# C scores over full rows with the low keys in both row halves, and the first pass's bias rows read three weight loads later

## What is computed

```python
h = jnp.einsum('bsd,de->bse', x, w_in)
a_out = pool_mixer(a_v, a_group_w, a_scale) * jax.nn.silu(a_gate)
b_out = swa_sink_attention(b_q, b_k, b_v, b_sinks) * jax.nn.silu(b_gate)
c_out = chunk_relbias_attention(c_q, c_k, c_v, c_rel_bias) * jax.nn.silu(c_gate)
y = jnp.einsum('bse,ed->bsd', jnp.concatenate([a_out, b_out, c_out], -1), w_out)
x = layer_norm(alpha * x + y)
```

```python
s = jnp.einsum('bnqhd,bnkhd->bnhqk', qc, kb) * (C_HEAD_DIM ** -0.5)
s = jnp.where(valid, s + bias, NEG_INF)
o = jnp.einsum('bnhqk,bnkhd->bnqhd', softmax(s), vb)
```

## Time and profile before

| | us |
|---|---|
| median of 3 runs | 3065.4 |
| profiled execution, its own time | 3064.84 |
| its span, first to last instruction | 3063.1 |
| TensorE busy | 2966.9 (97%) |
| VectorE busy | 1396.8 (46%) |
| ScalarE busy | 1202.5 (39%) |
| GpSimd busy | 1285.9 (42%) |
| mean granted clock of TensorE | 0.986 |

### The profile page before, as it was taken

The page is one execution under the profiler, slowest core; times in us unless marked ns, Lnnn a source line. Parts: engine busy times, 40 slices in busy tenths (PEclk is TensorE's granted clock), DMA queues, the critical chain, the costliest instruction groups (busy, mean ns, idle before and its releaser), DMA issues.

```text
span 3063.1 us, 46760 instructions
## 1 busy us (share of the span) xinstructions
PE 2966.9 (97%) x14272; PEld 2459.6 (80%) x14272; DVE 1396.8 (46%) x2483; ACT 1202.5 (39%) x2543; POOL 1285.9 (42%) x942
## 2 busy tenths in 40 slices
PE   7999999999999999999999999999999999999995
PEld 6777888888777878888878788888887777888884
DVE  4343455422556555541155555552126556555204
ACT  4333445422433444542234344553224444444321
POOL 4333444444434334444444444444443343444445
PEclk9999999999999999999999999999999999999998
DMA  5323322354433322235444442224553343222343
GB/s 174 99 91 107 103 83 81 98 170 157 146 130 124 117 89 80 82 95 163 158 153 138 136 136 86 79 80 140 162 179 104 97 134 130 83 79 79 101 125 142
DMA packets 187768, 360.68 MB, mean 118 GB/s; under 512 B 19072, under 2 KB 27296, under 8 KB 184352
## 3 DMA queue, kind: packets, MB, share of 16 engines
q1 hardware_dynamic: 185952, 346.99, 36.3%
q10 hardware_dynamic: 1728, 12.58, 1.0%
HBM read 319.63 MB, written 43.02 MB: 118 GB/s over the span
## 4 chain that ended last, share of the span: by engine, by line
PE 89%; issue 5%; DVE 4%; ACT 1%; POOL 1%; DMA 0%; SPq 0%; POOLq 0%; ACTq 0%; DVEq 0%
PE acc L510 58%; PE sc L510 17%; PE pv L510 11%; DVE res L1315 2%; PE sc L572 2%; DVE res L1320 1%; PE sc L618 1%; ACT mixl L807 1%; POOL last_sums L1145 0%; DVE mixl L1187 0%; POOL last_sums L1147 0%; DVE mixh L1187 0%; PE acc L540 0%; ACT mixh L807 0%; PE pv L534 0%
## 5 line engine op out<-in xcount | busy, mean ns | idle before, releaser
L1138 POOL TENSOR_TENSOR wl<-raw,wh 128x512 fp32r<-128x512 f32 x928 | 1263.5, 1366 | 1757.6 <-ACT wh L807 1753.7
L510 PE MATMUL acc<-xh,wh 128*128 128x512 f32 x2624 | 1048.4, 400 | 37.0 <-POOL wl L1138 25.1
L510 PE MATMUL acc<-xh,wl 128*128 128x512 f32 x2624 | 1032.2, 393 | 0.0
L510 PE MATMUL acc<-xl,wh 128*128 128x512 f32 x2624 | 1031.8, 393 | 0.0
L807 ACT ACTIVATE wh<-raw 128x512 fp32r<-128x512 f32 x931 | 576.0, 629 | 1029.2 <-PE acc L510 667.9
L510 PEld LDWEIGHTS acc<-xh,wh 128*128 128x128 f32 x2624 | 499.4, 190 | 139.9 <-POOL wl L1138 30.7
L510 PEld LDWEIGHTS acc<-xh,wl 128*128 128x128 f32 x2624 | 498.0, 190 | 107.8
L510 PEld LDWEIGHTS acc<-xl,wh 128*128 128x128 f32 x2624 | 499.4, 190 | 97.0
L510 PE MATMUL sc<-wh,mixh 128*128 128x512 f32 x512 | 199.6, 390 | 0.0
L510 PE MATMUL sc<-wh,mixl 128*128 128x512 f32 x512 | 199.4, 389 | 0.0
L510 PE MATMUL sc<-wl,mixh 128*128 128x512 f32 x512 | 199.2, 389 | 0.0
(11 more groups left out here) (178 smaller groups left out, 3788.2 us busy)
## 6 DMA issues: line engine op xcount, KB each, us to landing
raw<-in_wall SPq DMA_DIRECT2D x931, 256.0 KB, 2.6
res_scratch<-res ACTq DMA_DIRECT2D x12, 1024.0 KB, 3.9
res<-res_scratch SPq DMA_DIRECT2D x12, 1024.0 KB, 6.0
res<-in_x SPq DMA_DIRECT2D x8, 1024.0 KB, 5.3
x_scratch<-res SPq DMA_DIRECT2D x8, 1024.0 KB, 4.2
prob<-x_scratch SPq DMA_DIRECT2D x32, 256.0 KB, 3.3
res<-x_scratch SPq DMA_DIRECT2D x8, 1024.0 KB, 5.6
hist_scratch<-mixh SPq DMA_DIRECT2D x8, 768.0 KB, 4.0
```

The source lines that it names most:

```text
L510: return nc.tensor.matmul(o, lhsT, rhs, start=start, stop=stop)
L1138: nc.gpsimd.tensor_tensor(wl[:, s, :], raw[:, s, :], wh[:, s, :].bitcast(F32), ALU.subtract).then_inc(w_lo, 1)
```

## The change

There are two edits.

The low keys get the layout of the high keys: `ck_l` becomes a pair of tiles, `ck_l[h]` with head h's low keys in both halves of the rows. The low-key matmul of a head then runs over all 128 rows with the same query tile as the high-key matmul (so it also adds low query by low key), and stands right behind it: head 0 high and low, head 1 high and low. VectorE writes two more pieces of 64 rows by 512 for each pair in each pass, and the history kept for the next pass grows from 5 to 6 tiles. For the B heads the helper only replaces a loop that did the same.

In pass 0 the read of the bias rows, with its two waits, moves from step 5 to step 8 of SyncE's loop.

```diff
-        hist_d = nc.dram_tensor("hist_scratch", (C_PAIRS, P, 5, 512), F32, kind="Internal").ap()
+        hist_d = nc.dram_tensor("hist_scratch", (C_PAIRS, P, 6, 512), F32, kind="Internal").ap()
-        ck_l = mixh[:, MIX_B + 4:MIX_B + 6, :].rearrange("p a n -> p (a n)")
+        ck_l = [m[:, MIX_B + 4:MIX_B + 6, :].rearrange("p a n -> p (a n)") for m in (mixh, mixl)]
...
-                            for m, a, b in ((mixh, 0, 3), (mixl, 3, 5)):
+                            for m, a, b in ((mixh, 0, 3), (mixl, 3, 6)):
...
-                        if s == (10 if it else 5):
+                        if s == (10 if it else 8):
...
                     for h in range(2):
                         mm(sc[h][:, a:b], cq[h][:, qs], ck[h][:, ks], True, False)
-
-                    for h in range(2):
-                        last = mm(sc[h][:, a:b], cq[h][ROWS[h], qs], ck_l[ROWS[h], ks], False, True)
+                        last = mm(sc[h][:, a:b], cq[h][:, qs], ck_l[h][:, ks], False, True)
                         if b == end:
                             last.then_inc(cs_full, 1)
...
             def keys_lo(o, whole, hi):
                 for h in range(2):
-                    last = lo(o[ROWS[h], :], whole[ROWS[h], :], hi[h][ROWS[h], :])
+                    for rows in ROWS:
+                        last = lo(o[h][rows, :], whole[ROWS[h], :], hi[h][ROWS[h], :])
                 return last
...
-                    keys_lo(ck_l[:, HALF:2 * HALF], acc[0], [k[:, HALF:2 * HALF] for k in ck]).then_inc(k_ok, 1)
+                    keys_lo([k[:, HALF:2 * HALF] for k in ck_l], acc[0], [k[:, HALF:2 * HALF] for k in ck]).then_inc(k_ok, 1)
```

More of the change, by code:

```diff
@@ L1433, in _ @@
                 dv.wait_ge(qh_ok, QS * it + C_PAIRS + 2)
[L1434 to L1437, removed]
+                keys_lo([k[:, HD:] for k in bkl], s0[:, 0:HALF], [k[:, HD:] for k in bk]).then_inc(bq_ok, 1)
                 dv.wait_ge(vh_ok, (C_PAIRS + 1) * (it + 1))
```

## The result

The changed kernel takes 3043.1 us (median of 4 runs, 3041.0 to 3044.4), the kernel before beside it 3065.7 (4 runs, 3063.5 to 3067.2): a ratio of 0.9925 [0.991, 0.9941], 22.6 us less. The forecast was 3061.5 with a range of 3053 to 3070, so the time lies 10 us under the range. What it said of TensorE's work and of the bias read came out, and the clock took less than booked. VectorE's two pieces, booked at 16.8 us, lengthened the waits by 2.6 and cost about 5 when added alone.

A forecast was written before the change was run, and what follows sets the result against it. TensorE, busy 97% of the span, was taken as the bound. From 3064.84 us, minus 24.2 for scores, plus 16.8 for VectorE's pieces and 3.8 for the clock, gave 3061.2; forecast 3061.5 us for the median, range 3053 to 3070.

The forecast's parts named there:

- the bias read: SyncE in pass 0: moving the read gains nothing, since the bias transfer itself holds up the weight load.
- the clock: TensorE after the 12 waits: one slow stretch at 1.2 GHz behind each, a loss of 3.8 us.
- VectorE's two pieces: VectorE in passes 1 to 3: two more pieces lengthen each of 12 TensorE waits by 1.4 us, 16.8 us lost.
- TensorE's scores: Score matmuls on TensorE: gaps around 64-row pairs go away, a gain of 24.2 us.
- the doubt about 128 columns: First-half score blocks: 128-column matmuls may not keep their columns' pace, so 0.9 us a pair taken, not 0.99.
- The third rival: VectorE's pieces are hidden and cost nothing, giving 3041 us; chance 0.03.
- rows 4: Trace of VectorE before the change, passes 1 to 3: no gap from the keys to the queries' low part.
- The first rival: TensorE's scores: full rows lose side-by-side time if over 0.14 of 0.41 us a group stays; 3099 us, chance 0.05.

The follow-up runs named there:

- added alone: Kernel before plus VectorE's two more key pieces, scores still 64-row matmuls side by side, bias read at the sixth load: 3071.4 us, ratio 1.0016.
- half rows in turn: Changed kernel with low-key matmuls again over 64 rows, one behind each full-row one, never side by side: 3127.1 us, ratio 1.021.
- two pieces behind the layer norm: Kernel before plus two 64-row by 512 pieces on VectorE, put after the layer norm instead of ahead of it: 3097.0 us, ratio 1.01.
- full rows heads apart: Changed kernel with the high keys of both heads first, then the low keys of both: 3042.5 us, ratio 0.9933.
- the two cheap moves: Against the changed kernel: layer norm's scaling ahead of the wait for keys, 3011.1 us; bias rows written by row, 3006.4 us; both, 2975.9 us.

## Why the prediction was wrong

**TensorE's scores: right.** 24.2 us were booked. The block of 320 columns came to 1.29 us and not 1.25, so 0.49 less a block and not 0.53; the block of 512 came to 0.91 as said. In the first halves it was 0.83 a pair and not 0.9: the doubt about 128 columns was right, that block gave 0.18 for the 0.33 of its columns. That makes 15.7 + 6.6 = 22.3. The fixed cost around a 64-row pair is that of changing the number of rows, 0.19 to 0.2 a change on average, as the kernel with half rows in turn showed.

**VectorE's two pieces: the step that failed.** "two more of the same shape and sources (PSUM and SBUF) put everything behind them 1.4 us later" took the duration of what stands behind them as given. It isn't: 4.32 us for the scaling, read as its own cost in the earlier trace rows, was about 1.9 us of work (four of 0.53, each starting 0.08 before the one ahead ends) and 2.4 of standing beside GpSimd. The 1.4 us later start gave 1.2 of it back. Measured 2.6 us of waits against 16.8. The runs show both sides: two such pieces behind the scaling cost 16.8 in waits, the term as it was booked.

**The third rival, pieces hidden (3041), had the number and the wrong reason.** It was given 0.03 "against it: no gap in rows 4". There is no gap, and the pieces are paid for; they were offset, not hidden. A rival should have been written for the instructions that stood in between: 1138 ns a scaling instruction on average, 532 ns at best, in the trace of before.

**The clock: smaller than booked.** 3.8 us were booked, for a slow stretch behind every wait; there are five behind the 12 waits and two new ones elsewhere, which makes about 1.6. The waits stayed at 2.1 us instead of the 3.3 that the term was built on. Where they did reach 3.3, in the kernel with two pieces behind the layer norm, the loss came: 15 us of its 31.8 are not waits. But half rows in turn had a slow stretch behind all twelve at waits of 2.1 us, so that the changed kernel has only five isn't explained by the short waits alone; this stays open.

**The bias read: right.** It was put at nothing, and measured at 0.9997 [0.9988, 1.0006]. What holds pass 0 is the transfer that writes the bias rows, as the earlier trace rows were read; that it does so by running on few of the engines was not said.

**The first rival, full rows lose the side by side: refuted** by the block's 1.29 us, by full rows heads apart and by half rows in turn. Its condition was also mis-stated: by the forecast's own 0.53 a block, 0.27 of the 0.41 us a group would have to stay before the gain is gone, and not 0.14.

**The sum.** With the measured terms it is 3064.8 - 22.3 + 2.6 + 1.6 = 3046.7, against 3044.4 for the profiled execution. The forecast was 16.8 us too high for that execution (3061.2 - 3044.4): 14.2 of it is VectorE's term, 2.2 the clock's and 2.3 not placed, while TensorE's gain, 1.9 smaller than booked, went the other way.

## What to carry to other kernels

The duration of an instruction in a trace is that of its place: where an engine's minimum for a form is half its mean, find what stands beside it before adding work ahead of it, since moving it by 1.4 us changed it here by 1.2. Matmuls on half of the rows between full-row ones pay twice 0.2 us for the change, so putting the operand into both halves, though it adds a product (low by low) that isn't needed, was the cheaper way at every width here (0.17 to 0.27 us saved a block of one group). And where one transfer holds up a queue, look at how few engines it keeps busy: the two cheap moves found beside the change gave three times what the change did.

## What the runs showed of the hardware

- A 128x512 TENSOR_SCALAR in SBUF took 0.53 us alone and as much as 1.5 to 1.66 us beside GpSimd's TENSOR_TENSOR of SBUF tiles, and 0.53 too where it had begun before the split; four of them took 4.32, 3.12 or 2.42 us by the microseconds of overlap (3.3, 2.0, 1.0). VectorE's 64x512 pieces with one operand in PSUM took 0.68 to 0.70 us in both situations.
- Going from 128 rows to 64 or back cost TensorE about 0.2 us each time (0.41 us around a 64-row pair, 1.48 for eight changes); changing the PSUM tile at every matmul cost nothing that the trace shows (starts 0.14 to 0.15 apart in both orders).
- Waits as short as 0.9 us were followed by a slow stretch (1.2 GHz for 3.4 us), twice in the changed kernel and not at all at the same places before. Behind 12 waits of 1.8 to 2.1 us there were 5 or 6 slow stretches with full rows, 7 to 9 with 64-row pairs side by side and 12 with half rows in turn; behind those of 2.8 and 3.3 us there were 12. Which of the equal waits get one isn't settled by these runs.
- Two copies of 384 KB whose outer dimension is 2 kept DMA at 50 GB/s, and ScalarE waited 16.42 us for a load behind them; with 128 as the outer dimension DMA moved 168 GB/s in all, and the wait was 5.03.
